# Second model: the steps between sublayers reordered, the two last output panels taken tile by tile, the two streams split

## The reference, cut to what matters

```
h = modulate(rms_norm(x, g_pre[sub]), shift, scale)     # modulate: h * (1 + scale) + shift
y = swiglu(h, w1, w2)            # or the attention block with its own w_in and w_out
x = x + weight * gate * rms_norm(y, g_post[sub])
```

## Time and profile before

| | us |
|---|---|
| median of 3 runs | 3239.94 |
| lowest and highest of them | 3239.58, 3253.25 |
| the profiled execution, its own time | 3251.33 |
| its span in the trace | 3249.5 |
| mean granted clock of TensorE | 0.952 |
| TensorE busy | 2934.7 (90%) |
| VectorE, ScalarE, GpSimd busy | 1134.1 (35%), 704.5 (22%), 1257.1 (39%) |

### The profile page before, as it was taken

The page is one execution under the profiler, slowest core; times in us unless marked ns, Lnnn a source line. Parts: engine busy times, 40 slices in busy tenths (PEclk is TensorE's granted clock), DMA queues, the critical chain, the costliest instruction groups (busy, mean ns, idle before and its releaser), DMA issues.

```text
span 3249.5 us, 41524 instructions
## 1 busy us (share of the span) xinstructions
PE 2934.7 (90%) x16084; PEld 2425.5 (75%) x16084; DVE 1134.1 (35%) x1705; ACT 704.5 (22%) x1331; POOL 1257.1 (39%) x531
## 2 busy tenths in 40 slices
PE   8989789999897999599997888999979999788797
PEld 7967568789675786488886777788868888676696
DVE  2823733237237232500224263200340013425336
ACT  3432111134221211210112142210131111213211
POOL 4700000057000000366664503466645666562586
PEclk9999989999998999799999977999989999899899
DMA  6555431344554312322221202122222223230353
GB/s 225 182 207 225 190 130 40 130 173 173 218 220 181 130 41 103 124 98 93 101 92 67 89 1 65 65 97 93 101 78 79 102 90 103 66 116 27 105 179 129
DMA packets 67459, 383.89 MB, mean 118 GB/s; under 512 B 19072, under 2 KB 20736, under 8 KB 21888
## 3 DMA queue, kind: packets, MB, share of 16 engines
q1 hardware_dynamic: 66464, 379.19, 32.6%
q10 hardware_dynamic: 864, 2.84, 0.2%
HBM read 380.96 MB, written 1.05 MB: 118 GB/s over the span
## 4 chain that ended last, share of the span: by engine, by line
issue 30%; POOL 10%; POOLq 9%; PE 4%; DMA 2%; DVE 1%; SPq 1%; ACT 1%; DVEq 0%; ACTq 0%
POOL m_ws L1645 9%; POOLq L1644 7%; DMA m_ring<-in_panels 2%; PE m_bank L1752 1%; POOL m_ws L1663 1%; POOLq L1657 1%; SPq L1598 1%; POOLq L1662 1%; PE m_bank L1904 0%; PE m_bank L1689 0%; DVE m_ws L2146 0%; PE m_bank L1690 0%; PE m_bank L1691 0%; PE m_bank L1882 0%; PE m_bank L1869 0%
## 5 line engine op out<-in xcount | busy, mean ns | idle before, releaser
L1689 PE MATMUL m_bank<-m_aT,m_ws 128*128 128x512 f32 (+1 forms) x1664 | 604.0, 363 | 21.9 <-POOL m_ws L1645 6.3
L1690 PE MATMUL m_bank<-m_aT_low,m_ws 128*128 128x512 f32 (+1 forms) x1664 | 601.6, 362 | 0.0
L1691 PE MATMUL m_bank<-m_aT,m_ws 128*128 128x512 f32 (+1 forms) x1664 | 601.4, 361 | 0.0
L1645 POOL TENSOR_TENSOR m_ws<-m_ring,m_ws 128x2048 fp32r<-128x2048 f32 x127 | 592.6, 4666 | 18.7
L337 POOL TENSOR_TENSOR m_ws<-m_ring,m_ws 128x2048 fp32r<-128x2048 f32 x48 | 221.0, 4613 | 596.8 <-ACT m_ws L806 596.8
L1752 PE MATMUL m_bank<-m_ws,m_hs 128*128 128x512 f32 x1848 | 422.5, 390 | 4.3 <-POOL m_ws L1663 1.5
L1752 PEld LDWEIGHTS m_bank<-m_ws,m_hs 128*128 128x128 f32 x1848 | 346.1, 188 | 80.0 <-issue 7.6
L1689 PEld LDWEIGHTS m_bank<-m_aT,m_ws 128*128 128x128 f32 x1664 | 315.9, 190 | 73.6 <-issue 18.1
L1691 PEld LDWEIGHTS m_bank<-m_aT,m_ws 128*128 128x128 f32 x1664 | 316.1, 190 | 47.7
L1690 PEld LDWEIGHTS m_bank<-m_aT_low,m_ws 128*128 128x128 f32 x1664 | 316.1, 190 | 47.0
L1656 POOL TENSOR_TENSOR m_small<-m_small 128x1 f32<-128x1 f32 x158 | 32.8, 208 | 821.2 <-PE m_bank L1691 455.4
(11 more groups left out here) (355 smaller groups left out, 4002.9 us busy)
## 6 DMA issues: line engine op xcount, KB each, us to landing
m_ring<-in_panels SPq DMA_DIRECT2D x352, 1024.0 KB, 4.9
m_bias<-in_rpb SPq DMA_DIRECT2D x48, 64.0 KB, 2.4
m_hT<-in_ln_rows ACTq DMA_DIRECT2D x2, 1024.0 KB, 7.9
m_con<-in_con SPq DMA_DIRECT2D x1, 1408.0 KB, 12.4
m_memT<-in_memT SPq DMA_DIRECT2D x1, 1024.0 KB, 5.6
x_tok<-in_x SPq DMA_DIRECT2D x1, 1024.0 KB, 14.3
m_ctx_tok<-in_ctx SPq DMA_DIRECT2D x1, 1024.0 KB, 5.0
out<-x_tok SPq DMA_DIRECT2D x1, 1024.0 KB, 4.0
```

Of the source, the lines that this page charges most:

```text
L1645: nc.gpsimd.tensor_tensor(ws[:, p, 1, :], ring[:, p, :], ws[:, p, 0, :].bitcast(F32), ALU.subtract)\
L1689: mm(out, w, a, start=start, stop=False)
L1690: mm(out, w, a_low, start=False, stop=False)
L1691: return mm(out, w_low, a, start=False, stop=stop)
```

## The change

The second model's seams are written anew. What it does:

- **Last two panels.** `last_panels` takes the place of `last_panel`: for each tile the four chunks of the two last panels run one after the other, 24 matmuls, before the next tile begins. It waits for the split of both panels first. The first of the two counts as used after the second chunk of the last tile.
- **Seam.** `transition` takes the place of `norm_out` and `norm_in` on ScalarE and VectorE. Both go tile by tile in an order written out by hand: output and input of tile 0, the same of tile 1, then the outputs of tiles 2 and 3 with the main stream's evictions in between, then the context. `inverse` takes the place of `refine`, with one tile (128 x 1) and scalar operations in place of products of two tensors.
- **Split of the activations.** ScalarE evicts straight into `aT`; VectorE's `low` reads PSUM again (`scalar_tensor_tensor`), subtracts `aT`, and adds the shift in a second operation. The cast and the eviction to `hidT` go.
- **Streams.** Transposes of the main stream go to banks 0 to 3, of the context to banks 4 to 7. `lead` runs the first two panels with the main stream first (256 columns a matmul), the context's transposes between the units of the second panel, and then both panels with the context. The first panel counts as used after its context part; where the first panels need no context, at once.
- **Row sums.** `diag` is made last, and `row_sums` runs behind `lead` in a feed-forward network and behind the fourth input panel in an attention block; with two tiles out it has 4 matmuls in place of 8. ScalarE copies the result behind two swishes.
- In `hidden` the first two panels no longer wait on `h_free`.

GpSimd's and SyncE's lists are not changed. The core of the diff:

```diff
+            def transposed(e, st):
+                pe.wait_ge(s["xn_in"], IN_TILES[e] + NT * st + NT)
+                for j in range(KD // 2):
+                    for k in (2 * j, 2 * j + 1):
+                        for i in range(NT):
+                            last = nc.tensor.transpose(bank[:, 4 * st + j, ...], y[:, NT * st + i, k * P:(k + 1) * P], ident)
+                    last.then_inc(s["xn_ps"], 1)
+            def row_sums(e):
                 pe.wait_ge(s["diag_in"], e + 1)
-                for st in range(2):
+                pe.wait_ge(s["aT_split"], KD * IN_STREAMS[e + 1])
+                for st in range(SUBS[e][3] // NT):
...
+            def stream_of(e, b, b0, st, units, least):
...
                 for k in range(KD):
-                    pe.wait_ge(s["aT_split"], KD * e + max(k, 1) + 1)
+                    pe.wait_ge(s["aT_split"], KD * (IN_STREAMS[e] + st) + max(k + 1, least))
+                    for u in units:
+                        last = parts(bank[:, b0 + u, at], ..., aT[:, k, at], aT_low[:, k, at], k == 0, k == KD - 1)
+            def lead(e, n0, second):
...
+                transposed(e, 0)
+                split(0)
+                last = stream_of(e, b[0], 0, 0, (0, 1), KD // 2)
+                if not second:
+                    last.then_inc(s["used"], 1)
+                split(1)
+                stream_of(e, b[1], 2, 0, (0,), KD)
+                if two:
+                    transposed(e, 1)
+                last = stream_of(e, b[1], 2, 0, (1,), KD)
+                if not second:
+                    last.then_inc(s["used"], 1)
+                else:
+                    for p in range(2):
+                        stream_of(e, b[p], 2 * p, 1, (0, 1), 0).then_inc(s["used"], 1)
...
-            def last_panel(w, a, a_low, tiles, first_chunk=None):
+            def last_panels(w, a, a_low, tiles, chunk=None):
                 for i in range(tiles):
-                    for k in range(2):
-                        last = rows_tile(i, w[:, 0, k, :], w[:, 1, k, :], a[k], a_low[k], False, k == 1)
+                    done = i == tiles - 1
+                    for k in range(4):
+                        last = rows_tile(i, w[k // 2][:, 0, k % 2, :], w[k // 2][:, 1, k % 2, :], a[k], a_low[k], False, k == 3)
+                        if done and k % 2 == 0 and chunk:
+                            last.then_inc(s[chunk], 1)
+                        elif done and k == 1:
+                            last.then_inc(s["used"], 1)
+                    last.then_inc(s["used" if done else "acc_in"], 1)
...
-                one(FF // 2 - 2, 0)
-                n = n0 + FF // 2 - 1
-                pe.wait_ge(s["split_in"], n + 1)
+                n = n0 + FF // 2 - 2
+                pe.wait_ge(s["split_in"], n + 2)
...
 ScalarE:
+            def transition(e, last_panel=None):
...
+                for i in range(NT):
+                    if outs:
+                        square_out(e - 1, i, last_panel)
+                    if ins:
+                        square_in(e, i)
+                if outs > NT:
+                    for i in range(NT, 2 * NT):
+                        square_out(e - 1, i, last_panel)
+                if ins > NT:
+                    high(e, 0, 0, 2)
+                    square_in(e, 2)
+                    high(e, 0, 2, 4)
+                    square_in(e, 3)
+                    high(e, 1, 0, 4)
...
 VectorE:
+            def inverse(r, total):
+                t, u = small[:, 48:49], small[:, 50:51]
+                V.tensor_scalar(t, total, 1.0 / D, 1e-6, ALU.mult, ALU.add)
+                V.reciprocal(r, r)
+                dve.drain()
+                V.tensor_scalar(u, r, r, t, ALU.mult, ALU.mult)
+                dve.drain()
+                V.tensor_scalar(u, u, -0.5, 1.5, ALU.mult, ALU.add)
+                dve.drain()
+                V.tensor_scalar(r, r, u, None, ALU.mult)
...
+            def low(e, st, j0, j1):
...
+                    for k in (2 * j, 2 * j + 1):
+                        V.scalar_tensor_tensor(hidT[:, k, at], bank[:, 4 * st + j, ...], gsc[...], aT[:, k, at].bitcast(F32),
+                                               ALU.mult, ALU.subtract)
                     dve.drain()
+                    for k in (2 * j, 2 * j + 1):
+                        V.tensor_scalar(aT_low[:, k, at], hidT[:, k, at], modv[...], None, ALU.add)
+            def transition(e):
...
+                for i in range(NT):
+                    if outs:
+                        residual(e - 1, i)
+                    if ins:
+                        normed(e, i)
+                if outs > NT:
+                    residual(e - 1, 2)
+                if ins:
+                    low(e, 0, 0, 2)
+                if outs > NT:
+                    residual(e - 1, 3)
+                if ins:
+                    low(e, 0, 2, 4)
+                if ins > NT:
+                    normed(e, 2)
+                    normed(e, 3)
+                    low(e, 1, 0, 4)
+                if ins:
...
```

More of the change, by code:

```diff
@@ L1728, in hidden @@
             def hidden(n0, e, f, tokens):
-                for p in range(2):
-                    pe.wait_ge(s["split_in"], n0 + p + 1)
-                    if n0 == SHARED:
-                        pe.wait_ge(s["split_dve"], p + 1)
-                    pe.wait_ge(s["h_free"], f * FF + p + 1)
-                    if p == 0:
-                        first_unit_panel(e, n0 % 2, (tokens, tokens)).then_inc(s["used"], 1)
-                    else:
-                        unit_panel((n0 + 1) % 2, 2, (tokens, tokens)).then_inc(s["used"], 1)
+                lead(e, n0, tokens > T)
+                row_sums(e)
                 with pe.Fori(1, FF // 2) as g:
@@ L1927, in _ @@
                     last.then_inc(s["used"], 1)
+                pe.wait_ge(s["split_in"], n0 + 14)
+                last_panels([ws[:, (n0 + n) % 2, :, :].rearrange("p h (k c) -> p h k c", k=2) for n in range(2)],
+                            [aT[:, 4 + k, :] for k in range(4)], [aT_low[:, 4 + k, :] for k in range(4)], tiles)
                 e += 1
@@ new lines, in square_in, with high @@
+            def square_in(e, i):
+                if e:
+                    act.wait_ge(s["x_new"], NEW_X[e - 1] + i + 1)
+                a_(y[:, i, :], tok(i), ACT.Square, accum_out=small[:, i:i + 1])
+                act.drain()
+                a_(small[:, 4 + i:5 + i], small[:, i:i + 1], ACT.Sqrt, bias=eps, scale=1.0 / D).then_inc(s["sd_in"], 1)
+            def high(e, st, j0, j1):
+                l, sub = SUBS[e][0:2]
+                for j in range(j0, j1):
+                    act.wait_ge(s["xn_ps"], 4 * (IN_STREAMS[e] + st) + j + 1)
+                    for k in (2 * j, 2 * j + 1):
+                        last = a_(aT[:, k, st * T:(st + 1) * T], bank[:, 4 * st + j, (k % 2) * T:(k % 2 + 1) * T], ACT.Identity,
+                                  scale=gsc[:, 3 * l + sub, k, st:st + 1], bias=modv[:, l, 3 * sub, k, st:st + 1])
+                    last.then_inc(s["aT_in"], 1)
@@ new lines, in transition @@
+            def transition(e, last_panel=None):
+                outs = SUBS[e - 1][3] if e else 0
+                ins = SUBS[e][2] if e < len(SUBS) else 0
+                a_(small[:, 62:63], eps, ACT.Sqrt)
+                for i in range(NT):
[12 more added lines that the diff above has]
+                    high(e, 1, 0, 4)
+                elif ins:
+                    high(e, 0, 0, 4)
@@ L1946, in norm_in, with row_copies @@
+            def row_copies(e):
                 act.wait_ge(s["rows_ps"], e + 1)
-                for st in range(2):
+                for st in range(SUBS[e][3] // NT):
                     for hf in range(2):
@@ L1984, in high_hidden @@
                        .rearrange("p o t -> p (o t)"), ACT.Copy).then_inc(s["hs_in"], 1)
-                with act.Fori(0, FF // 2 - 1) as g:
+                for p in range(2):
+                    swish(p, 0)
+                row_copies(e)
+                with act.Fori(1, FF // 2 - 1) as g:
                     for p in range(2):
@@ new lines, in residual @@
+            def residual(e, i):
+                halves = lambda x: x.rearrange("p (h c) -> p h c", h=2)
+                dve.wait_ge(s["ysd_in"], NEW_X[e] + i + 1)
+                if i == 0:
+                    dve.wait_ge(s["rows_in"], e + 1)
+                inverse(small[:, 12 + i:13 + i], small[:, 8 + i:9 + i])
+                out = bank[:, 2 * i:2 * i + 2, :]
+                V.scalar_tensor_tensor(out, out, small[:, 12 + i:13 + i], halves(rows[:, i // 2, :]), ALU.mult, ALU.mult)
+                dve.drain()
+                V.tensor_tensor(halves(tok(i)), halves(tok(i)), out, ALU.add).then_inc(s["x_new"], 1)
@@ new lines, in transition @@
+            def transition(e):
+                outs = SUBS[e - 1][3] if e else 0
+                ins = SUBS[e][2] if e < len(SUBS) else 0
+                for i in range(NT):
[16 more added lines that the diff above has]
```

(6 more changed lines are left out.)

169 lines of the change are left out of this document (61 added, 108 removed).

## The result

| | before | changed |
|---|---|---|
| median, on the same chips | 3246.6 us (6 runs, 3234.07 to 3257.56) | 3278.64 us (6 runs, 3259.4 to 3286.89) |
| ratio, 95% interval | | 1.0091 (1.006 to 1.0122) |
| profiled execution, its span | 3251.33, 3249.5 us | 3259.4, 3257.6 us |

The change makes the kernel 0.9% slower, about 30 us. The forecast of 3239 us (no change) was wrong; the measured time lies in the range of 3205 to 3282.

What follows compares the result with a forecast made beforehand. TensorE's waits at the seams, 99.3 us of them for `diag`, stood out; between seams TensorE bounds with four tiles, GpSimd's splitting with two. The places summed to +0.6 us saved against the median of 3239.94: 3239 us, range 3205 to 3282.

Steps and rivals of the forecast that it cites:

- entry: Entry of the second model: panel 0 starts slow, lead and rows end at 1372.2 against 1370.8 before; -1.4 us.
- seam 1: First seam between sublayers: 7.5 us saved after the last output matmul, less 7.3 wait and 2.1 clock; -1.9 us.
- seam 3: Third seam between sublayers: 9.6 us saved after the last output matmul, less 7.2 wait and 2.1 clock; +0.3 us.
- seam 4: Fourth seam: the chain of panel splits moves up with panel 0, saving 17.5 us, less 9.4; +8.1 us.
- seam 5: Seam with two tiles: 8.6 us saved, less 5.4 for held-back panel work, 2.1 clock and 1 for rows; 0.
- end: End of the model: last panels 5.2 us later, clock 2.1, one tile's residual left instead of two +2.5; -4.8 us.
- The wait for both splits and the clock behind it: Before the last two panels, seams 1 to 4: TensorE idles 7.0 to 7.3 us, then loses 2.1 at low clock.
- Rival D: Last two panels: the last split is ahead of need, so waits and clock loss vanish; 3187 us, chance 0.05.
- the seam's chain behind t: After t, the end of a seam's last output matmul: first dense matmul at t + 7.8; 9.6 us saved at seams 2, 3.
- The row sums: `rows` moved into the dense part: 8 matmuls at 0.44 us, 3.5 us no longer hidden under VectorE's work.
- Rival C: Seams: the 128x1 scalar operations of `inverse` are held up by GpSimd's splits; +40 us, 3279 us, chance 0.20.
- Rival B: Seams: VectorE's adds slip between GpSimd's operations and the clock returns at once or never falls; 3213 us, chance 0.22.

Runs made afterwards that it cites:

- e1: The changed kernel with the last two panels in the old order, each panel's split waited for on its own; 3241.7 us.
- e2: The changed kernel with `low` scaling and shifting in the PSUM bank, then subtracting `aT` from the bank; 3268.4 us.
- e4: The changed kernel with the products of `inverse` as one tensor by another again, on 128 x 1; 3321.5 us in one run.
- e6: The changed kernel with three tiles of the second-to-last panel ahead of the wait for the last panel's split; 3243.5 us.
- e8: The changed kernel with the second-to-last panel for tiles 0, 1, 2, last for 0, 1, second-to-last for 3, last for 2, 3; 3252.7 us.
- e5: The changed kernel with the edits of e2 and e6 together; 3244.0 us.

## Why the prediction was wrong

The first profile of the changed kernel is its fastest execution, by this attention part (18.1 us shorter than in the second) and the first model (4.4 us shorter). The second has 157.0 us there, the profile of before 156.2, so these two are compared: 3284.11 less 3251.33, 32.8 us, like the medians. Each row is read from one end of a stretch to the next, so the first row holds the first model too. Positive is saved; "last panels" stands against the forecast's wait and clock, and the rest is what comes behind t.

| place | forecast | measured | of it last panels | of it behind t |
|---|---|---|---|---|
| entry | -1.4 | -1.3 | | |
| seam 1 | -1.9 | -10.5 | -10.3 (forecast -9.4) | -0.2 (forecast +7.5) |
| seam 2 | +0.3 | -4.3 | -10.2 (-9.3) | +5.9 (+9.6) |
| seam 3 | +0.3 | -4.8 | -10.0 (-9.3) | +5.2 (+9.6) |
| seam 4 | +8.1 | +1.9 | -9.3 (-9.4) | +11.2 (+17.5) |
| seam 5 | 0 | -8.3 | -12.8 (-7.5) | +4.6 (+7.6) |
| end | -4.8 | -5.3 | -7.7 (-7.3) | +2.4 (+2.5) |
| sum | +0.6 | -32.6 | | |

- **The wait for both splits and the clock behind it: right.** Forecast 7.0 to 7.3 and 2.1 at seams 1 to 4; the wait was 7.27 at seams 1, 3 and 4 and 7.03 at seam 2, and the step grew by 9.0 to 10.4 in two profiles. e1 took it away and gained 37 us. At the end it was -7.7 for -7.3. Rival D (the panels don't wait) is out.
- **The failed step is the seam's chain behind t**, and in it the sentence "the adds wait for GpSimd (until 4.9 and 7.3), so j = 0, 1 are ready at 7.8". The sum lets the additions wait until t + 4.9 and t + 7.3, about where the first split and the short operation of the second end, and charges nothing for the second's long operation (4.61 us), which comes right behind. In seam 3 the first pair ended at t + 7.2; the second, issued at t + 8.0, met that long operation, which ran from t + 6.9 to t + 11.5, and ended at t + 11.9. Residual 3, queued behind it on VectorE, moved with it. With the additions free (e2) seam 3 gives 59.4 - 49.8 = 9.6 and seam 2 gives 59.35 - 49.4 = 10.0, where the forecast had 9.6 twice (by other terms in part, as said at e2). Four seams at some 4 us make 16 of the 33 us missed. Smaller parts of the rest are in the points below.
- **Seam 1 has a second miss.** GpSimd's small operation ahead of the third panel's split ran 2.73 us instead of 0.19, beside VectorE's bias additions (1536 columns, two SBUF inputs), and TensorE then stood for 3.82 us, where the forecast had 1.5:

```profile
1748.13 3.42 DVE L2293 TENSOR_TENSOR m_bias<-m_bias,m_con 128x1536 f32<-128x1536 f32 x2
...
1748.88 2.73 POOL L1656 TENSOR_TENSOR m_small<-m_small 128x1 f32<-128x1 f32 x1 [21.88 <-PE m_bank L1691]
...
1758.37 0.79 PE L1689 MATMUL m_bank<-m_aT,m_ws 128*128 128x512 f32 x1 [3.82 <-POOL m_ws L1645]
```

  The prediction charged 2 us for these additions at seam 4 and left them out at seam 1. In e2 they met GpSimd at another moment, and the cost stayed: the small operation took 0.46 us, but the two of the split behind it 3.23 and 5.81, where 1.90 and 4.51 stand in the changed kernel, and TensorE stood for 4.2 us.

```profile
1741.59 0.46 POOL L1656 TENSOR_TENSOR m_small<-m_small 128x1 f32<-128x1 f32 x1 [17.77 <-PE m_bank L1691]
...
1742.20 3.23 POOL L1643 TENSOR_SCALAR m_ws<-m_ring 128x2048 fp32r<-128x2048 f32 x1 [0.16 <-issue]
1745.58 5.81 POOL L1645 TENSOR_TENSOR m_ws<-m_ring,m_ws 128x2048 fp32r<-128x2048 f32 x1
```

- **Seam 4**: direction and mechanism right (the chain of splits moves up with the first panel), 11.2 of 17.5; e2 gives 15.0, so 2.5 stay unexplained.
- **Seam 5**: the wait was forecast at 5.4 + 2.1. Read from the use of the panel two before the last, as at the other seams, the step grew from 12.8 to 21.0 us, 8.2, so this term was near. The -12.8 of the table is read from the use of the last V panel; the other 4.6 lie in the attention part in between, whose length scatters (99.5 to 107.2 us from there to t in the eight kernels without the wait), so no run here lays them to the change. Behind t the chain of two tiles gave 4.6 for 7.6. e2 did not mend that (2.8). The trace of the changed kernel shows two terms of it: the scaling of tile 0 took 2.28 us beside GpSimd's split, where the forecast had 0.75, and the 16 transposes took 3.67 us at the low clock, where the earlier trace rows have 1.91. Together they are 3.3 us, as much as the 3.0 that is missing; no run takes them away one by one, so this is read, not tested.

```profile
3017.73 1.90 POOL L1661 TENSOR_SCALAR m_ws<-m_ring 128x2048 fp32r<-128x2048 f32 x1 [0.16 <-issue]
3017.89 2.28 DVE L2181 TENSOR_SCALAR m_y<-x_tok,m_small 128x1024 f32<-128x1024 f32 x1
...
3027.62 3.67 PE L1699 MATMUL m_bank<-m_con,m_y 128*128 128x128 f32 x16 [12.35 <-DVE m_y L2181]
```

- **The entry** matches by luck. The first model, which no edit touches, ended 1.8 us later in this profile (1303.8 for 1302.0). From there to the use of the third panel the kernel before takes 80.0 us and the changed one 79.4 in both profiles: 0.6 saved, where the forecast had 1.4 lost.
- **The row sums** came in as forecast: the stretch from the third panel's use to the sixth's in layer 0's attention grew by 3.45 (forecast 3.5).
- **Rival C** named the right neighbour and the wrong operation. It gave 3279 us, and 3278.6 was measured, but by another way: the 128 x 1 operations of `inverse` were never held (0.276 us at most in the changed kernel). e4 shows what they would have cost in the old form. The Trainium skill (SBUF — State Buffer, who interferes with whom) holds that a scalar operation contends with GpSimd only in a two-port mode, and one with two SBUF inputs whenever GpSimd's operation reads SBUF. The trace agrees with the second half (4.34 us at most for one element), and with the first if a single element is in no such mode, which no trace shows by itself: the last product took 0.216 us at most in the scalar form, while scalar operations on 128 x 2, 128 x 256 and 128 x 1024 took up to 4.46, 3.79 and 5.05.
- The same section of the Trainium skill says that a VectorE operation with at most one SBUF input, outside those modes, does not contend. e2 agrees: 0.427 us at most in 88 times.
- **Rival B** (the seam freer) fell: the additions were held, the first dense matmul came at t + 12, not t + 5, and the clock was low in every seam.

## What to carry to other kernels

Before an order is changed, list for the busiest neighbour on the shared SBUF path (here GpSimd's 7 us splits) which of the other engine's operations will now lie beside it, and charge each with the whole rest of the neighbour's operation, not with its own time. What held in every order tried here was a change of the form or the engine of the operation (PSUM as source, a scalar operand for a single element, ScalarE); moving it in time freed the additions in e6 and e8 but put the scaling in their place. Work that finishes earlier is worth only what the chain behind it can use: three tiles early by up to 8 us bought 3 us with the additions held and 7 with them free, for a 9 us wait.

## What was not expected

- The split of layer 0's attention into two durations, 137 to 142 us in five and 155 to 157 us in nine of the fourteen profiles, with the same instructions: in the long ones the granted clock stands near 0.5 for 55 to 58 us with TensorE busy 28 to 30 of 30 us. At 15 to 18 us it is as large as half the effect that was studied. The times of one kernel fall into groups that would fit it (e5: 3218.8 to 3227.3 three times, 3240.5 to 3247.7 seven times), but only one execution of each kernel has a trace. What decides it stayed open.
- The block works both ways: beside VectorE's additions of 1536 columns GpSimd's 128 x 1 operation of 0.19 us took 2.73, and in e2 its operation of 1.90 us took 3.23.
- An operation that is not the longest can be the worst: at seam 3 of e4, 4.1 us were lost twice to products of one element for each partition.
